# Rotation of the dilated heads moved from VectorE to GpSimd, their transposes moved one attention unit later

## The chip, the cores and the metric

The kernel runs on one core of a Trainium2 chip. The metric is the device time of one execution in microseconds, as the median of several executions. Five engines work side by side, each through its own list of instructions: TensorE (PE in the profile), VectorE (DVE), ScalarE (ACT), GpSimd (POOL) and SyncE (SP, which here only issues transfers). They meet through semaphores: an instruction with a wait holds up all that is queued behind it on its engine.

## What is computed

Two blocks on a sequence of 256 tokens and 1024 channels in float32. The change lies in the first, which has two layers. Of each layer the part that matters is this (cut from the reference):

```python
for layer in range(DEPTH):                      # DEPTH = 2
    h = rmsnorm(x, norm_mix[layer])
    z = h @ w_in[layer]                         # 256 x 2964
    ...                                         # z is split into the inputs of four mixers
    o_a = nsa_mixer(...); o_b = diff_mixer(...); o_c = mlstm_mixer(...)
    o_d = dilated_mixer(heads(d_q), heads(d_k), heads(d_v), cos64, sin64)
    x = x + jnp.concatenate([o_a, o_b, o_c, o_d], axis=-1) @ w_out[layer]
    ...                                         # feed-forward part

def dilated_mixer(q, k, v, cos, sin):
    q = apply_rope(q, cos, sin)                 # x1*cos - x2*sin, x1*sin + x2*cos
    k = apply_rope(k, cos, sin)
    ...                                         # masked attention with counted keys
```

The second block (convolutions, routing, experts) is not touched.

## The kernel before

The 256 tokens are two tiles of 128 rows. z is made in six pieces (chunks) of up to 512 columns. For each, TensorE multiplies both tiles; ScalarE takes tile 0 out of PSUM (`z_act`) and VectorE takes tile 1 (`z_dve`). The last piece, `C_DIL`, holds the queries and keys of the dilated mixer: 2 x 4 heads of 64 columns.

Attention is a software pipeline over 14 units, `u` = 0 to 13: 4 to 7 are the differential mixer, 8 and 9 the window part of the NSA mixer, 10 and 13 its compressed part, 11 and 12 the dilated mixer (`U_DIL` = 11). There is no scheduler: the order on each engine is that of the code. In step `u`

- TensorE transposes the probabilities of unit u (L585, L587; waits `probs` and `o_done` of the unit before), does a piece of other work in `ahead_of_values` (products of z, L522, and from step 9 on the output product, L618), multiplies by the values (L602), makes the scores of unit u+2 (L570), and does `behind_scores`;
- ScalarE copies the transposed probabilities of unit u+1 out of PSUM (`transposed_out`, L867 to L871) and takes the exponentials of unit u+2 (L856);
- VectorE turns exponentials into the factors of unit u+1 (`probabilities`, L1096 to L1133), takes the output of unit u (`unit_out`, L1146 to L1157) and masks the scores of unit u+2 and finds their maxima (`masked`, L1046 to L1051).

The dilated heads take a way through all of them. VectorE rotates tile 0 of them at the end of step 6 and tile 1 at the end of step 7, in `rotate_dil` (L381 to L386, four instructions per tile), and raises `rope`. TensorE transposes them behind the scores of step 8 (`dil_batch`, eight transposes at L545, waiting for `rope`), and ScalarE copies the result out of PSUM at the end of its step 8 (`qk(B_DIL, ...)`, L839) and raises `prep_ev`. The scores of unit 11, made in step 9, wait for that copy.

GpSimd has little to do in this stage: it rotates the heads of the differential mixer (`rotate_diff`, the same function `rotate` with the same 128x512 sizes) when their piece of z is there, and then waits for the end of attention to issue small transfers (`ada_bias`, `params`).

Of the kernel before, what the change touches and what calls it, by code (L numbers as in the profile page):

```python
# [394 lines left out]
def first_pool(nc, pool, m, a):  # L395
# [28 lines left out]
    def rotate_diff(L):  # L424
# [7 lines left out]
            last = rotate(nc.gpsimd, pool, m, m.rz_b, m.tmp_pool, i, [(z_heads(m, i, Z_BQ, 16, 32), 0, 16, 32)])  # L432
        last.then_inc(s["rope_b"], 1)

    params(0)
    pool.wait_ge(m.consts_in, 16 * m.n_consts)
    for L in range(DEPTH):
        rotate_diff(L)
        ada_bias(L)
        if L < DEPTH - 1:  # L440
            params(L + 1)
# [51 lines left out]
def first_tensor(nc, pe, m):  # L493
# [5 lines left out]
    for L in range(DEPTH):  # L499
# [203 lines left out]
        def dil_batch():  # L703

            pe.wait_ge(s["rope"], nth(L, "rope", 3))
            pe.wait_ge(s["OT"], nth(L, "OT", 1))
            pairs(batch(B_DIL), [cols(m.rz_d, k * P) for k in range(4)]).then_inc(s["prep_ps"], 1)

        def ahead_of_values(u):

            if u < 4:
                z_part(C_VALUES, u // 2, u % 2)
            elif u < 8:
                z_part(C_DIL, u // 2 - 2, u % 2)
            elif u == 8:
                pe.wait_ge(s["o_final"], nth(L, "o_final", 1))
                out_transposes(0)
            elif u == 9:
                pe.wait_ge(m.ring_full[5], (L * 2 + 2) * 16)
                pe.wait_ge(m.ring_full[2], (L * 2 + 2) * 16)  # L720
                z_taken(C_DIL)
                out_ready(0)
                out_part(0, 4)
            elif u == 10:
                pe.wait_ge(s["prep_ev"], nth(L, "prep_ev", N_PREP))
                out_part(1, 4)
            elif u == 11:
                out_ready(1)
                out_part(0, 2)
            elif u == 12:  # L730
                out_part(1, 2)
            else:
                out_ready(2)
                out_part(0, 0)
                out_transposes(3)

        def behind_scores(u):

            if u == 1:
                diff_batch()  # L740
            elif u == 2:
                cmp_batch()
            elif u == 3:
                kv_batch()
            elif u == 8:
                dil_batch()
            elif u == 10:
                pe.wait_ge(s["o_final"], nth(L, "o_final", 2))
                out_transposes(1)
            elif u == 12:  # L750
                pe.wait_ge(s["masked"], nth(L, "masked", N_UNITS))
                out_transposes(2)
# [62 lines left out]
def first_scalar(nc, act, m):  # L815
# [5 lines left out]
    for L in range(DEPTH):  # L821
# [102 lines left out]
        for u in range(N_UNITS):  # L924
            if u == 1:
                z_out(C_VALUES)
            if u == 5:
                z_out(C_DIL)
                head_root(0)
            if u == 8:  # L930
                out_taken(0)
            if u == 9:
                head_root(1)
            if u == 10:
                out_taken(1)
            if u == 12:
                out_taken(2)
            if u + 1 < N_UNITS:
                transposed_out(u + 1)
            if u + 2 < N_UNITS:  # L940
                exponentials(u + 2)
            if u == 1:
                qk(B_DIFF, T_BQ, 4)
            if u == 2:
                rows = m.ps[0:CMP_ROWS, 6, 0:2 * HD].rearrange("n (a e) -> n a e", a=2)
                for x in range(2):
                    evac(B_CMP, m.cmp_u[0:CMP_ROWS, :, x, :], rows)
                evac(B_CMP, m.cmp_u[32:32 + CMP_ROWS, :, 0, :], m.ps[32:32 + CMP_ROWS, 6, 0:2 * HD].rearrange("n (a e) -> n a e", a=2)).then_inc(s["prep_ev"], 1)
            if u == 3:
                evac(B_KV, m.kcT[:, 0:N_CMP], m.ps[:, 6, 0:N_CMP])  # L950
                evac(B_KV, m.vc[0:N_CMP, :], m.ps[0:N_CMP, 7, 0:HD]).then_inc(s["prep_ev"], 1)
            if u == 8:
                qk(B_DIL, T_DQ, 4)
        out_taken(3)
        out_taken(4)

# [23 lines left out]
def first_vector(nc, dve, m):  # L980
# [8 lines left out]
    for L in range(DEPTH):  # L989
# [198 lines left out]
                last = tt(sub, sub, m.z[:, :, Z_O:Z_O + GW], ALU.mult)  # L1188
            last.then_inc(s["o_final"], 1)

        def rotate_dil(i):
            return rotate(v, dve, m, m.rz_d, m.tmp_dve, i, [(z_heads(m, i, Z_DQ, 8, HD), 0, 8, HD)])

        dve.wait_ge(s["small_ready"], nth(L, "small_ready", 1))
        probabilities(0)
        masked(1)
# [3 lines left out]
        for u in range(N_UNITS):  # L1200
            if u + 1 < N_UNITS:
                probabilities(u + 1)
            if u == 3:
                z_out(C_VALUES)
            if u == 7:
                z_out(C_DIL)
            unit_out(u)
            if u + 2 < N_UNITS:
                masked(u + 2)
            if u == 4:  # L1210
                sub_squared(0)
            if u == 5:
                sub_scaled(0)
            if u == 6:
                dve.wait_ge(s["z_act"], nth(L, "z_act", C_DIL + 1))
                rotate_dil(0)
            if u == 7:
                dve.drain()
                rotate_dil(1).then_inc(s["rope"], 1)
            if u == 8:  # L1220
                sub_squared(1)
            if u == 9:
                sub_scaled(1)
# [1410 lines left out]
```

## Time and profile before

| what | value |
|---|---|
| median of 3 runs | 2112.6 us (2111.42 to 2115.61) |
| the profiled execution | 2113.28 us, of which 2111.4 us are the span of the instructions |
| TensorE busy | 1957.8 us (93%) |
| VectorE busy | 658.9 us (31%) |
| ScalarE busy | 315.2 us (15%) |
| GpSimd busy | 84.9 us (4%) |
| granted clock of TensorE over the span | 0.975 of full speed |
| attention steps 6 to 13, layer 0 | about 130 to 190 us |
| the same, layer 1 | about 561 to 620 us |

The profile is of one execution. A span's start is time zero of every view. "Idle before" names the engine whose event ended a wait. A row that merges instructions gives the time from the first one's start to the last one's end, and neighbouring TensorE rows overlap by some tenths of a microsecond, since matmuls are pipelined.

### The profile page before, as it was taken

The numbers are of one execution on the slowest core, as the hardware profiler recorded it, in microseconds if no ns is written. First come the engines' busy times: TensorE is split into PE (matmuls) and PEld (weight loads), VectorE is DVE, ScalarE is ACT, GpSimd is POOL, SyncE is SP. The second block draws the span as 40 slices with busy tenths as digits, with TensorE's granted clock in tenths as the row PEclk, the third lists the DMA queues.
The fourth block names the chain that finished last, engine by engine and source line by source line (L and its number), as shares of the span: only waits on it lengthen the run. The fifth ranks groups of instructions, "written<-read, shape, count | busy, mean of one in ns | idle before, by whom it ended". The sixth has DMA issues, their size and how long they took to land.

```text
span 2111.4 us, 21989 instructions
## 1 busy us (share of the span) xinstructions
PE 1957.8 (93%) x8546; PEld 1080.5 (51%) x8546; DVE 658.9 (31%) x1270; ACT 315.2 (15%) x741; POOL 84.9 (4%) x127
## 2 busy tenths in 40 slices
PE   8988999999889999899999999999899998899886
PEld 4555777755557777674444434443684333233222
DVE  1463434324643433474311111111424211111103
ACT  2442000014430000203111011110101100000000
POOL 3102000001020000200000000000000000000000
PEclk9999999999999999999999999999999999999999
DMA  9215777643148786517699999999536799999995
GB/s 310 74 61 167 260 261 273 221 149 86 61 130 301 246 283 228 196 45 299 256 378 426 428 426 428 427 428 419 218 130 268 311 424 428 427 428 427 428 426 242
DMA packets 158898, 603.07 MB, mean 286 GB/s; under 512 B 16776, under 2 KB 73016, under 8 KB 128080
## 3 DMA queue, kind: packets, MB, share of 16 engines
q1 hardware_dynamic: 153728, 591.43, 71.8%
q0 software_dynamic: 4880, 10.22, 1.8%
q8 instruction: 69, 1.13, 0.2%
q14 instruction: 29, 0.24, 0.0%
q10 hardware_dynamic: 192, 0.05, 0.0%
HBM read 597.67 MB, written 1.10 MB: 284 GB/s over the span
## 4 chain that ended last, share of the span: by engine, by line
PE 73%; DMA 17%; DVE 5%; issue 2%; ACT 1%; DVEq 1%; ACTq 1%; SPq 0%
PE ps L1986 15%; PE ps L790 15%; DMA ring<-in_e_w_up 8%; DMA ring<-in_e_w_gate 7%; PE ps L796 7%; PE ps L522 7%; PE ps L2004 5%; PE ps L1820 4%; PE ps L1785 3%; PE ps L1914 3%; PE ps L1833 3%; PE ps L1929 3%; PE ps L618 2%; DMA ring<-in_e_w_down 1%; PE ps L587 1%
## 5 line engine op out<-in xcount | busy, mean ns | idle before, releaser
L790 PE MATMUL ps<-hT,ring 128*128 128x256 f32 x1408 | 314.1, 384 | 1.5 <-DVE hT L284 1.5
L790 PEld LDWEIGHTS ps<-hT,ring 128*128 128x128 f32 x1408 | 277.5, 198 | 34.1 <-issue 4.0
L1986 PE MATMUL ps<-ring,hT 128*64 128x512 f32 (+1 forms) x1024 | 231.3, 604 | 30.7 <-DMA ring<-in_e_w_up 15.8
L1986 PE MATMUL ps<-ring,late 128*64 128x512 f32 (+1 forms) x960 | 213.6, 597 | 20.0 <-DMA ring<-in_e_w_up 11.3
L2004 PE MATMUL ps<-ring,qkT 128*64 128x512 f32 (+1 forms) x1024 | 226.6, 594 | 5.8 <-ACT qkT L2201 4.5
L522 PE MATMUL ps<-ring,hT 128*128 128x512 f32 (+1 forms) x384 | 170.1, 594 | 3.1 <-DMA ring<-in_w_in 2.3
L1986 PEld LDWEIGHTS ps<-ring,hT 128*64 128x64 f32 (+1 forms) x1024 | 72.9, 125 | 185.2 <-issue 185.2
L796 PE MATMUL ps<-ring,late 128*128 128x512 f32 x352 | 154.7, 592 | 0.0
L1986 PEld LDWEIGHTS ps<-ring,late 128*64 128x64 f32 (+1 forms) x960 | 66.3, 124 | 160.9 <-issue 160.9
L2004 PEld LDWEIGHTS ps<-ring,qkT 128*64 128x64 f32 (+1 forms) x1024 | 68.6, 123 | 145.1 <-issue 145.1
L1269 DVE SCALAR_TENSOR_TENSOR qkT<-ring,cc,qkT 128x512 f32<-128x512 f32 x168 | 125.9, 749 | 10.3 <-issue 0.4
L2462 DVE TENSOR_TENSOR qkT<-ps,qkT 128x512 f32<-128x512 f32 (+1 forms) x64 | 44.2, 690 | 267.4 <-PE ps L2004 267.4
L522 PEld LDWEIGHTS ps<-ring,hT 128*128 128x128 f32 x384 | 73.1, 197 | 80.4 <-issue 70.7
L1290 DVE TENSOR_TENSOR late<-ps,late 128x256 f32<-128x256 f32 x44 | 18.7, 425 | 296.6 <-ACT late L972 296.6
L2483 DVE TENSOR_TENSOR qkT<-ps,qkT 128x512 f32<-128x512 f32 (+1 forms) x32 | 22.1, 690 | 280.8 <-PE ps L1986 280.8
L796 PEld LDWEIGHTS ps<-ring,late 128*128 128x128 f32 x352 | 66.9, 190 | 74.6 <-issue 73.7
L1914 PE MATMUL ps<-qkT 128*128 128x512 f32 x192 | 95.2, 618 | 0.0
L1929 PE MATMUL ps<-qkT,O 128*128 128x256 f32 x384 | 92.6, 381 | 2.1 <-DVEq L2443 2.1
L2479 DVE TENSOR_TENSOR x<-ps,x 128x1024 f32<-128x1024 f32 x24 | 29.4, 1225 | 196.5 <-PE ps L1914 196.5
L1820 PE MATMUL ps<-hT,ring 128*128 128x256 f32 x384 | 85.0, 384 | 1.6 <-DVE hT L2253 0.9
L972 ACT ACTIVATE late<-ps 128x256 f32<-128x256 f32 x44 | 16.9, 384 | 445.8 <-PE ps L790 445.8
L1929 PEld LDWEIGHTS ps<-qkT,O 128*128 128x128 f32 x384 | 70.3, 190 | 25.5 <-issue 14.6
(379 smaller groups left out, 1693.8 us busy)
## 6 DMA issues: line engine op xcount, KB each, us to landing
ring<-in_e_w_down SPq DMA_DIRECT2D x64, 2048.0 KB, 16.1
ring<-in_e_w_up SPq DMA_DIRECT2D x64, 2048.0 KB, 17.3
ring<-in_e_w_gate SPq DMA_DIRECT2D x60, 2048.0 KB, 17.1
ring<-in_ada_w SPq DMA_DIRECT2D x24, 2048.0 KB, 10.4
ring<-in_w_gate SPq DMA_DIRECT2D x22, 1024.0 KB, 7.5
ring<-in_w_up SPq DMA_DIRECT2D x22, 1024.0 KB, 9.9
ring<-in_w_down SPq DMA_DIRECT2D x22, 1024.0 KB, 11.7
ring<-in_w_in SPq DMA_DIRECT2D x8, 2048.0 KB, 14.3
```

Of the source, the lines that this page charges most:

```text
L522: last = mm(m.ps[:, 4 + i, 0:chunk_width(n)], m.hT[:, j, i * P:(i + 1) * P], w[:, j, :], start=(j == 0), stop=(j == KC - 1))
L790: last = mm(m.ps[:, c, at:at + SEQ], w[:, j, c, :], m.hT[:, j, :], start=(j == 0), stop=(j == KC - 1))
L796: last = mm(m.ps[:, 4 + 2 * i + n2, :], m.ucT[:, c, i * P:(i + 1) * P], wd[:, c, n2 * 512:(n2 + 1) * 512], start=(u == 0 and c == 0), stop ...
L1269: last = stt(acc, w, m.cc[:, j:j + 1], acc, ALU.mult, ALU.add)
L1785: last = mm(m.ps[:, c % 4, half * SEQ:(half + 1) * SEQ], w[half][:, j, at:at + P], m.hT[:, j, :], start=(j == 0), stop=(j == KC - 1))
L1820: last = mm(dst, w[half][:, j, at:at + P], m.hT[:, j, :], start=(j == 0), stop=(j == KC - 1))
L1833: last = mm(m.ps[:, 4 + 2 * i + n, :], vT[:, j, i * P:(i + 1) * P], w[:, j, :], start=(j == 0), stop=(j == KC - 1))
L1914: last = mm(m.ps[:, 6 + n, :], m.GwT[:, i, :], half_of(m.ye, n), start=True, stop=True)
L1929: last = mm(m.ps[:, k % depth, n * SLOTS:(n + 1) * SLOTS], hN, m.G[l][:, i].rearrange("p x s -> p (x s)"), start=(i == 0), stop=(i == 1))
L1986: last = mm(dst, xg[:, j, at + x * n_tok:at + (x + 1) * n_tok], w(x, j), start=(j == 0), stop=(j == KC - 1))
L2004: lasts[x] = mm(dst, m.hidT[:, j, rows + x * n_tok:rows + (x + 1) * n_tok], half_of(w(x, j), n), start=(j == 0), stop=(j == 3))
L2462: tt(half_of(m.ye[rows], n), m.ps[rows, 4 + n, :], half_of(m.gf[rows], n), ALU.mult).then_inc(t["ye"], 1)
```

## The change

GpSimd gets a function `rotate_dil`, which stands right behind `rotate_diff`: it waits for both tiles of the piece `C_DIL` and rotates tile 0 and tile 1. VectorE loses its eight instructions per layer in steps 6 and 7. TensorE does `dil_batch` in step 9 behind the first part of the output product and ahead of the values, instead of at the end of step 8. ScalarE copies its result in step 9 behind `head_root(1)` (the square root of the sums of squares of the differential output) and ahead of `transposed_out(10)`.

```diff
@@ first_pool
+    def rotate_dil(L):
+
+        pool.wait_ge(s["z_act"], nth(L, "z_act", C_DIL + 1))
+        pool.wait_ge(s["z_dve"], nth(L, "z_dve", C_DIL + 1))
+        for i in range(TILES):
+            last = rotate(nc.gpsimd, pool, m, m.rz_d, m.tmp_pool, i, [(z_heads(m, i, Z_DQ, 8, HD), 0, 8, HD)])
+        last.then_inc(s["rope"], 1)
...
     for L in range(DEPTH):
         rotate_diff(L)
+        rotate_dil(L)
         ada_bias(L)
@@ first_tensor
                 out_ready(0)
                 out_part(0, 4)
+                dil_batch()
...
-            elif u == 8:
-                dil_batch()
@@ first_scalar
             if u == 9:
                 head_root(1)
+                qk(B_DIL, T_DQ, 4)
...
-            if u == 8:
-                qk(B_DIL, T_DQ, 4)
@@ first_vector
-        def rotate_dil(i):
-            return rotate(v, dve, m, m.rz_d, m.tmp_dve, i, [(z_heads(m, i, Z_DQ, 8, HD), 0, 8, HD)])
...
-            if u == 6:
-                dve.wait_ge(s["z_act"], nth(L, "z_act", C_DIL + 1))
-                rotate_dil(0)
-            if u == 7:
-                dve.drain()
-                rotate_dil(1).then_inc(s["rope"], 1)
```

TensorE, from the scores made in step 8 to those made in step 9, before:

```order
L570 MATMUL ps<-kcT,qkT 128x15 [waits prep_ev,masked]
L570 MATMUL ps<-kcT,qkT 128x15 x3
L545 MATMUL ps<-ident,qkT 128x128 [waits prep_ev,OT,rope]
L545 MATMUL ps<-ident,qkT 128x128 x7
L587 MATMUL ps<-ident,ring 128x128 [waits probs,o_done]
L587 MATMUL ps<-ident,ring 128x128 x7
L618 MATMUL ps<-ring,hT 128x512 [waits z_dve,z_act,OT,ring_full2,ring_full5]
L618 MATMUL ps<-ring,hT 128x512 x3
L602 MATMUL ps<-z,ring 128x64 [waits pt]
L602 MATMUL ps<-z,ring 128x64 x7
L570 MATMUL ps<-qkT 128x128 [waits prep_ev,masked]
```

The same place in the changed kernel, where the lines stand nine further down (L554 is `dil_batch`, L596 the transposes of the probabilities, L627 the output product, L611 the values):

```order
L579 MATMUL ps<-kcT,qkT 128x15 [waits prep_ev,masked]
L579 MATMUL ps<-kcT,qkT 128x15 x3
L596 MATMUL ps<-ident,ring 128x128 [waits probs,o_done]
L596 MATMUL ps<-ident,ring 128x128 x7
L627 MATMUL ps<-ring,hT 128x512 [waits z_dve,z_act,OT,ring_full2,ring_full5]
L627 MATMUL ps<-ring,hT 128x512 x3
L554 MATMUL ps<-ident,qkT 128x128 [waits prep_ev,OT,rope]
L554 MATMUL ps<-ident,qkT 128x128 x7
L611 MATMUL ps<-z,ring 128x64 [waits pt]
L611 MATMUL ps<-z,ring 128x64 x7
L579 MATMUL ps<-qkT 128x128 [waits prep_ev,masked]
```

The eight transposes of the dilated heads moved behind those of the probabilities and the eight products.

ScalarE, from the last exponentials of unit 10 to the exponentials of unit 11, before:

```order
L856 ACTIVATE ring,small<-ring,small 128x15 x3
L839 ACTIVATE qkT<-ps 128x1024 [waits prep_ps]
L878 ACT_TABLE_LOAD
L878 ACTIVATE small<-small,eps 128x2x4 [waits ss]
L867 ACTIVATE ring<-ps 15x4x128 [waits pv,pt_ps]
L856 ACT_TABLE_LOAD [waits pt_ps]
```

And in the changed kernel (L847 is the copy, L886 the square root):

```order
L864 ACTIVATE ring,small<-ring,small 128x15 x3
L886 ACT_TABLE_LOAD
L886 ACTIVATE small<-small,eps 128x2x4 [waits ss]
L847 ACTIVATE qkT<-ps 128x1024 [waits prep_ps]
L875 ACTIVATE ring<-ps 15x4x128 [waits pv,pt_ps]
L864 ACT_TABLE_LOAD [waits pt_ps]
```

The copy of the dilated heads moved behind the square root.

## Rows read from the trace of the kernel before

**Rows 1.** Page, part 1: busy time, share of span, weight of TensorE.

```profile
PE 1957.8 (93%) x8546; PEld 1080.5 (51%) x8546; DVE 658.9 (31%) x1270; ACT 315.2 (15%) x741; POOL 84.9 (4%) x127
```

**Rows 2.** Chain of waits, layer 0, steps 7 to 9: start us, us, what.

```profile
139.58 0.69 DVE qkT L381
...
141.01 0.70 DVE qkT L386
...
142.39 1.35 PE ps L545 x8
...
149.44 1.75 PE ps L602 x16
...
151.28 0.42 DVE late L1153
```

**Rows 3.** Timeline of VectorE, layer 0: start us, us, engine line op, idle before.

```profile
134.81 0.75 DVE L1002 TENSOR_SCALAR z<-ps,small 128x512 f32<-128x512 f32 x1
...
141.80 0.18 DVE L1096 RECIPROCAL small<-small 128x4 f32<-128x4 f32 x1
142.05 0.16 DVE L1099 TENSOR_TENSOR small<-small,gates 128x4 f32<-128x4 f32 x1
...
142.80 0.43 DVE L1155 TENSOR_TENSOR O<-O,late 128x256 f32<-128x256 f32 x1
```

**Rows 4.** Timeline of ScalarE, layer 0, steps 7 to 9.

```profile
139.52 0.51 ACT L856 ACTIVATE ring<-ring,small 128x256 f32<-128x256 f32 x1 [1.62 <-DVE small L1051]
...
141.41 0.19 ACT L856 ACTIVATION_READ_ACCUMULATOR ring<-ring,small 128x1 f32 x1
...
147.76 1.02 ACT L839 ACTIVATE qkT<-ps 128x1024 f32<-128x1024 f32 x1
...
150.10 0.30 ACT L878 ACTIVATE small<-small,eps 128x8 f32<-128x8 f32 x1
```

**Rows 5.** Timeline of TensorE, layer 0.

```profile
89.30 1.09 PE L545 MATMUL ps<-ident,qkT 128*128 128x128 f32 x8
...
130.68 0.65 PE L587 MATMUL ps<-ident,ring 128*128 128x128 f32 x4 [2.56 <-DVE O L1146]
131.17 3.60 PE L522 MATMUL ps<-ring,hT 128*128 128x512 f32 x8
...
139.54 0.62 PE L570 MATMUL ps<-kcT,qkT 64*128 64x15 f32 x8 [0.49 <-DVE small L1051]
...
167.19 1.97 PE L587 MATMUL ps<-ident,ring 128*128 128x128 f32 x8 [2.43 <-DVE O L1157]
168.95 4.29 PE L618 MATMUL ps<-ring,hT 128*128 128x512 f32 x8
```

**Rows 6.** Windows: stretch, length, busy of PE, PEld, DVE, ACT, POOL, then PEclk.

```profile
143.00:143.50 0.50, 0.50 (x5) 0.50 (x3) 0.43 (x3) 0.00 (x0) 0.00 (x0) 0.53 0.86 350
...
146.00:146.50 0.50, 0.50 (x2) 0.34 (x1) 0.00 (x0) 0.50 (x2) 0.00 (x0) 0.55 0.00 0
```

**Rows 7.** Timeline of GpSimd: ends of its rotation, layer 0, then layer 1.

```profile
74.41 1.09 POOL L381 TENSOR_TENSOR qkT<-z,late 128x512 f32<-128x512 f32 x1 [36.61 <-DVE z L1002]
...
83.87 1.26 POOL L386 TENSOR_TENSOR qkT<-qkT 128x512 f32<-128x512 f32 x1
...
503.21 1.09 POOL L381 TENSOR_TENSOR qkT<-z,late 128x512 f32<-128x512 f32 x1 [309.58 <-DVE z L1002]
...
511.05 1.26 POOL L386 TENSOR_TENSOR qkT<-qkT 128x512 f32<-128x512 f32 x1
```

**Rows 8.** Timeline of VectorE: one instruction, beside GpSimd's rotation and behind it.

```profile
82.23 0.97 DVE L1046 TENSOR_TENSOR ring<-ring,late 128x512 f32<-128x512 f32 x1 [0.30 <-PE ps L570]
...
512.45 0.69 DVE L1046 TENSOR_TENSOR ring<-ring,late 128x512 f32<-128x512 f32 x1 [0.30 <-PE ps L570]
```

**Rows 9.** Timelines of layer 1: TensorE at the batch, VectorE at the output.

```profile
572.84 1.69 PE L545 MATMUL ps<-ident,qkT 128*128 128x128 f32 x8 [2.23 <-DVE qkT L386]
...
573.25 0.42 DVE L1155 TENSOR_TENSOR O<-O,late 128x256 f32<-128x256 f32 x1
```

## The prediction, made before the changed kernel was run

> **What bounds the kernel now.** The page's engine table comes first: TensorE is busy for 1957.8 of 2111.4 us and VectorE for 658.9 [rows 1]. So work taken off VectorE gains only where TensorE waits for it. The change touches one place of each of the two layers, and there I read the chain of waits. In layer 0 it goes through the second rotation on VectorE (139.58 to 141.71), then the eight transposes of the dilated heads (142.39), then TensorE's own work up to the end of the values (149.44 + 1.75), and from there to the output of unit 9 on VectorE (151.28) [rows 2]. The timelines of the engines show what runs beside that chain, and the windows show TensorE's clock. Layer 1 has the same pattern, 430.45 us later: transposes at 572.84 after the same wait [rows 9].
>
> **Rotation leaves VectorE.** Two tiles per layer; each takes 141.71 - 139.58 = 2.13 us [rows 2]. The first one I cost at nothing: behind it VectorE takes the last piece of z at 134.81, and TensorE only ends its product for it then. The second stands on the chain, so 2.1 us per layer seem to be for the taking. They are not. Beside it ScalarE takes the exponentials of unit 9, from 139.52 to 141.41 + 0.19 = 141.60 [rows 4]. VectorE needs them for the factors of unit 9, which it begins at 141.80 [rows 3]; a handover from one engine to the next I take at 0.09 us, as between the end of the values (149.44 + 1.75 = 151.19) and the output at 151.28 [rows 2], so without the rotation they begin at 141.69. The gain for what follows on VectorE is **0.11 us**.
>
> **TensorE's work moves later.** Before, TensorE ends the scores of unit 10 at 139.54 + 0.62 = 140.16 [rows 5] and waits for the rotation until 142.39 [rows 2]. The transposes of the dilated heads then fill the rest of the time until VectorE has taken the output of unit 8, at 142.80 + 0.43 = 143.23 [rows 3], for which the transposes of the probabilities wait. In the changed kernel those come first, so TensorE starts when that output is there: 143.23 - 0.11 + 0.09 = **143.21**, against 142.39. All of its work from here to the end of the values is the same, in another order: 8 + 8 transposes, 8 products, 16 products with values. Nothing in it waits (below), so the end moves by as much as the start, **+0.82 us** at an equal clock. In layer 1 the output of unit 8 ends at 573.25 + 0.42 = 573.67 [rows 9], the start is 573.65 against 572.84, so +0.81.
>
> **The clock makes that a little less, or more.** TensorE's granted clock falls to its lower level (1.2 of 2.4 GHz, 0.53 as a mean of the half microsecond) at about 143.0 after the wait, and is low until about 146.4, where the mean is 0.55 [rows 6]. If the low stretch keeps its place, start time lost inside it counts half: layer 0 loses 0.64 at full clock up to 143.03 and half of 0.18 behind it, together 0.7; layer 1, where the eight transposes took 1.69 instead of 1.09 [rows 5, 9] and so ran low almost from their start, 0.5. Together 1.2 us in place of 1.6. But the wait grows from 2.2 to 3.0 us. A fall is no matter of course: a wait of 2.56 us at 130.68 is followed by products at full pace (3.60), one of 2.43 at 167.19 by transposes of 1.97 and products of 4.29 [rows 5]. A fall costs 4.29 - 3.60 + 1.97 - 1.09 = **1.6 us**. This place pays it already in both layers; executions in which it does not will mostly pay it after the change. I add nothing for it in the sum and 1.6 us per layer in the range.
>
> **GpSimd beside VectorE.** GpSimd starts when VectorE has taken the last piece of z, 134.81 + 0.75 [rows 3], plus the handover, at 135.65. The same rotation took it 85.13 - 74.41 = 10.72 us in layer 0 and 512.31 - 503.21 = 9.10 in layer 1 [rows 7]. So it ends between 144.8 and 146.4, and it overlaps the factors and the output of unit 8 on VectorE. The nearest row for what that costs: a VectorE instruction with two operands in SBUF took 0.97 us beside a GpSimd instruction and 0.69 when GpSimd had finished [rows 8], so 0.28. On the new path two such instructions stand in a row: the factors times the gates (142.05) and the sum into O (142.80) [rows 3]. Bounds for each: nothing, and the longest GpSimd instruction, 1.26 us [rows 7]. I take 0.28 for each, the one row there is, 0.56 per layer, partly in the low clock: **+0.4 us** per layer. The maskings of steps 7 and 8 have one operand in PSUM; that they aren't slowed is assumed, and no row shows it.
>
> The Trainium skill, "SBUF — State Buffer", section "Who interferes with whom", says that a VectorE instruction with two SBUF inputs contends with a GpSimd instruction that reads SBUF, and that whichever comes second blocks until the first is done. This trace agrees in direction with its 0.28 us; how long a full block is, no row shows. Taken at its word, two blocks per layer could come to 2.5 us, which is the slower rival below.
>
> **Does the new place make anybody wait?** TensorE reaches the moved transposes after the output product. Before, the values began at 149.44 [rows 2], with the transposes already done; 1.09 us of them [rows 5] now stand there instead. TensorE reaches them at 149.44 + 0.73 - 1.35 = 148.8 at the earliest (1.35 is what they took before). GpSimd is done by 146.4: a cover of 2.4 us. ScalarE's copy must be there before the scores of unit 11, which follow the values. ScalarE is through with the exponentials of unit 10 by 147.7; the square root takes until 150.40 - 148.78 = 1.62 us later, 149.3, and shifts with the rest by under 1 us; the transposes end at 150.0 to 151, and the values behind them at 151.8 to 152.8; the copy takes 1.02 [rows 4], while TensorE does the values for 1.75. That leaves 0.7 to spare, so nothing. GpSimd's next jobs wait for the end of attention and aren't late; SP's queue is passed by nothing.
>
> **Sum.** Layer 0: 0.7 + 0.4; layer 1: 0.5 + 0.4; together **+2.0 us**. From 151.28 on the chain of waits goes to the end of attention with no gap that a shift of this size could fill, and the feed-forward stage behind it is TensorE's, so the shift stays. The profiled execution's 2113.28 would be 2115.3; it lies 0.7 above the median of 2112.6, so the median is forecast at **2114.5 us** (2112.6 + 2.0, rounded to a half).
>
> **Rivals.**
> - The rotation's time is gained: the chain itself speaks for it, as it goes through the second rotation and 0.68 us behind it. Then 2 x 2.2 = 4.4 us go, 2108.2. Against it are the exponentials, which end 0.11 us before the rotation. Chance 0.04.
> - The clock is kinder: the later start shifts every following wait of TensorE, and some that now end in a fall of the clock (167.19) no longer do. One fall less is -1.6 us, two -3.2: 2111.3 to 2112.9. For it: the 2.56 us wait without a fall. Against it: it may as well go the other way. Chance 0.14.
> - Slower: GpSimd blocks VectorE for whole instructions at both places. The start of TensorE moves from 143.21 by 1.26 + 1.09 [rows 7] to 145.56, a loss of 3.2 us per layer at full clock (the low stretch then lies behind the start as well), 6.4 in both: 2119.0. It decides from 2112.6 + 4.2, so from 2.1 us per layer, which is 1.3 us of blocking over the two instructions. For it: GpSimd is busy in most of that stretch. Against it: the one such row shows 0.28. Chance 0.12.
> - GpSimd comes too late for the transposes: it would have to take over 13 us instead of 9.1 to 10.7, and each further microsecond costs one per layer. With 3 us more, 2112.6 + 2.0 + 2 x 0.5 to 2 x 1.5, 2115.5 to 2117.5. Chance 0.05.
>
> **How the numbers follow.** The forecast has 0.65. A measurement of this kernel can tell about 0.2% (4.2 us) from no change, as the three runs before spread over that much. The forecast, the kind clock and most of the late GpSimd lie within it: 0.83. Slower holds the blocking rival and a tail of the late one and of clock falls on top of the forecast: 0.13. Faster holds the first rival: 0.04. The range goes from the kind clock with one or two falls less, 2111.2, to just short of the blocking rival, which includes one fall more on top of the forecast plus the spread, 2117.8.
>
> **What would show it.** In the profile of the changed kernel: VectorE idle between its maxima of step 7 and the factors of unit 9, released by ScalarE (about 2.2 us); TensorE's wait ahead of the transposes of step 9 at 3.0 us or more, released by the sum into O; the moved transposes and the scores of unit 11 with no wait; the output of unit 9 beginning 0.7 to 1.5 us later than before; GpSimd's rotation 9 to 11 us long. Wrong I am if the factors or the sum into O of step 8 take over 1 us each, if TensorE waits for GpSimd or for ScalarE's copy, or if the output of unit 9 comes earlier than before.

## The result and the profile after

The changed kernel is slower by a quarter of a per cent: its median is 2117.6 us (15 runs, 2114.26 to 2122.72) against 2112.6 us of the kernel before, 1.0023 times as long, with an interval of 1.0016 to 1.0031. A second measurement, made with the last experiments, gave the same: 2118.25 us against 2112.28, 1.0023 (1.0015 to 1.0032). The forecast was 2114.5 us. The time lies in the range, at its upper edge; the sign is the one forecast; the size, 5.0 us instead of 2.0, is not.

The engine table after the change, in the columns of [rows 1]:

```profile
PE 1968.1 (93%) x8546; PEld 1083.8 (51%) x8546; DVE 652.2 (31%) x1254; ACT 314.9 (15%) x741; POOL 98.6 (5%) x143
```

GpSimd took over sixteen instructions (x127 to x143, 13.7 us), VectorE has sixteen fewer, and TensorE is busy for 10.3 us more **with the same 8546 instructions**. That is the first thing to see: the same instructions took longer, and the windows below show them at a lower clock. But 7.0 of the 10.3 us lie in the second block (1141.4 us busy before, 1148.5 after), whose length hardly changed (1241.0 and 1241.2 us); the sum over the span does not say what the change costs.

The chain of waits at the changed place of layer 0 (start, us, what), to be laid beside [rows 2]:

```profile
142.23 0.88 DVE O L1162
...
143.16 1.97 PE ps L596 x8
145.12 5.31 PE ps L627 x8
150.44 0.87 PE ps L554 x8
151.31 1.75 PE ps L611 x16
```

The second rotation has left the chain, as was meant. In its place stands the sum into O of unit 8 on VectorE, and the eight products of L627 take 5.3 us of it. The timeline of TensorE there (start, us, engine, line, operation, idle before), to be compared with [rows 5]:

```profile
139.11 0.62 PE L579 MATMUL ps<-kcT,qkT 64*128 64x15 f32 x8 [0.48 <-DVE small L1058]
143.16 1.97 PE L596 MATMUL ps<-ident,ring 128*128 128x128 f32 x8 [3.43 <-DVE O L1162]
144.92 5.52 PE L627 MATMUL ps<-ring,hT 128*128 128x512 f32 x8
150.27 1.04 PE L554 MATMUL ps<-ident,qkT 128*128 128x128 f32 x8
```

and the same stretch in the kernel before:

```profile
142.39 1.35 PE L545 MATMUL ps<-ident,qkT 128*128 128x128 f32 x8 [2.23 <-DVE qkT L386]
143.54 1.91 PE L587 MATMUL ps<-ident,ring 128*128 128x128 f32 x8
145.24 4.20 PE L618 MATMUL ps<-ring,hT 128*128 128x512 f32 x8
```

The wait grew from 2.23 to 3.43 us and the products from 4.20 to 5.52 (eight of the same size take 3.60 at full clock, [rows 5]). The windows give the clock (stretch, length, busy us of PE, PEld, DVE, ACT and POOL, then PEclk, the granted clock), here of the changed kernel:

```profile
141.50:142.00 0.50, 0.00 (x0) 0.00 (x0) 0.41 (x2) 0.36 (x1) 0.45 (x1) 0.95 1.14 363
142.00:148.50 6.50, 5.34 (x13) 3.27 (x14) 3.73 (x12) 3.26 (x10) 0.82 (x1) 0.50 0.44 173
148.50:149.00 0.50, 0.50 (x3) 0.18 (x2) 0.13 (x1) 0.49 (x2) 0.00 (x0) 0.73 0.00 0
...
575.50:578.50 3.00, 2.52 (x9) 2.10 (x10) 2.31 (x6) 0.52 (x1) 0.14 (x1) 0.50 0.69 281
578.50:579.00 0.50, 0.50 (x2) 0.33 (x1) 0.00 (x0) 0.50 (x2) 0.00 (x0) 0.65 0.00 0
```

In layer 0 TensorE was at its lower level (0.50, 1.2 of 2.4 GHz) from 141.95 to 148.77: a mean of 0.95 over half a microsecond is 0.05 us of it low, one of 0.73 is 0.27. That is 6.8 us, where the kernel before had 3.4, from 143.03 to 146.45 [rows 6]. In layer 1 the fall comes at 575.44 and the rise at 578.85, 3.4 us, as before.

The same happens a second time, further down in layer 1, at a wait whose length did not change. Changed kernel:

```profile
600.52 1.97 PE L596 MATMUL ps<-ident,ring 128*128 128x128 f32 x8 [2.43 <-DVE O L1164]
602.28 5.53 PE L627 MATMUL ps<-ring,hT 128*128 128x512 f32 x8
```

Kernel before:

```profile
597.64 1.97 PE L587 MATMUL ps<-ident,ring 128*128 128x128 f32 x8 [2.44 <-DVE O L1157]
599.40 4.11 PE L618 MATMUL ps<-ring,hT 128*128 128x512 f32 x8
```

**Where the 5.3 us between the two spans (2116.7 and 2111.4) are.** I measure from the start of one row to the start of another, in both profiles. "At the place" is from the scores of unit 10 to the output of unit 9. "Low" is for how long the granted clock was 0.50 in the stretch, before and after.

| stretch | before | after | difference | low |
|---|---|---|---|---|
| at the place, layer 0 | 11.74 | 14.04 | +2.30 | 3.4, 6.8 |
| at the place, layer 1 | 11.73 | 12.67 | +0.94 | 3.4, 3.4 |
| masking of unit 11 to first feed-forward product, layer 1 | 47.90 | 49.31 | +1.41 | 6.1, 11.5 |
| first feed-forward product of layer 1 to TensorE's first work of the second block | 239.99 | 240.74 | +0.75 | 4.1, 5.5 |
| ahead of the place, layer 0 | 139.54 | 139.11 | -0.43 | 10.2, 6.8 |

Together 4.97; the stretches that are left add 0.3, none of them more than that. The second profile of the changed kernel (r1_after, below) gives 14.05, 12.67, 49.30 and 240.76. The second profile of the kernel before (r2_before) has 11.72, 11.73, 47.97 and 240.08, so these four do not hang on one execution.

Other stretches do. From the first piece of z of layer 1 to the scores of unit 10 the kernel before took 127.16 us in one profile, with 10.2 us of low clock, and 124.18 in the other, with 3.4. And in layer 0, from the masking of unit 11 to the first feed-forward product, r2_before took 49.50 us where the first profile of the same kernel took 47.95 and the changed kernel 47.80 and 47.85. So the kernel before meets the lengthening of the third row too, only in the other layer and not in every execution. The wait is again that of step 11 (r2_before):

```profile
167.26 1.97 PE L587 MATMUL ps<-ident,ring 128*128 128x128 f32 x8 [2.44 <-DVE O L1157]
169.02 5.71 PE L618 MATMUL ps<-ring,hT 128*128 128x512 f32 x8
```

### The profile page after: what moved, and what is told of

It reads as the page before. It is cut to its first block, busy times and chain, and to the rows that moved or that the text cites. A ratio compares the mean times of both kernels' runs of the same rounds, so it can differ in the third digit from the quotient of the medians.

```text
span 2116.7 us, 21989 instructions
## 1 busy us (share of the span) xinstructions
PE 1968.1 (93%) x8546; PEld 1083.8 (51%) x8546; DVE 652.2 (31%) x1254; ACT 314.9 (15%) x741; POOL 98.6 (5%) x143
## 4 chain that ended last, share of the span: by engine, by line
PE 73%; DMA 17%; DVE 5%; issue 2%; ACT 1%; DVEq 1%; ACTq 1%; SPq 0%
PE ps L1984 16%; PE ps L798 15%; DMA ring<-in_e_w_gate 11%; PE ps L804 7%; PE ps L531 7%; PE ps L2002 5%; DMA ring<-in_e_w_up 4%; PE ps L1818 4%; PE ps L1783 3%; PE ps L1912 3%; PE ps L1831 3%; PE ps L1927 3%; PE ps L627 2%; DMA ring<-in_e_w_down 1%; PE ps L611 1%
## 5 line engine op out<-in xcount | busy, mean ns | idle before, releaser
L1984 PE MATMUL ps<-ring,hT 128*64 128x512 f32 (+1 forms) x1024 | 237.4, 618 | 25.5 <-DMA ring<-in_e_w_up 13.7
```

The lines of the kernel that those rows point to most:

```text
L1984: last = mm(dst, xg[:, j, at + x * n_tok:at + (x + 1) * n_tok], w(x, j), start=(j == 0), stop=(j == KC - 1))
```

## The experiments

Each was compared with the kernel before on the same chip, in 8 to 12 runs. "Place" is the length at the place in layer 0 and layer 1, 11.74 and 11.73 us before. "Low" is how long the granted clock was 0.50 there, added up from windows of half a microsecond or one.

| kernel | median us | before us | ratio and interval | place us | low us |
|---|---|---|---|---|---|
| e1_engine | 2115.7 | 2112.0 | 1.0020 (1.0011 to 1.0029) | 12.64, 12.59 | 3.4, 3.4 |
| e2_order | 2119.0 | 2112.0 | 1.0032 (1.0022 to 1.0041) | 12.97, 13.97 | 6.8, 6.8 |
| e3_psum | 2117.2 | 2112.0 | 1.0022 (1.0013 to 1.0031) | 12.20, 12.46 | 3.4, 3.4 |
| e4_warm | 2111.1 | 2112.0 | 1.0000 (0.9991 to 1.0009) | 11.33, 11.30 | 0, 0 |
| e5_warm_before | 2110.1 | 2112.7 | 0.9990 (0.9981 to 0.9999) | 10.11, 10.11 | 0, 0 |
| e6_warm_order | 2113.1 | 2112.7 | 0.9997 (0.9987 to 1.0007) | 10.99, 10.99 | 0, 0 |
| f1_fill_dve | 2110.4 | 2112.7 | 0.9992 (0.9981 to 1.0003) | 8.74, 8.73 | 0, 0 |
| f2_fill_pool | 2111.2 | 2112.7 | 0.9992 (0.9981 to 1.0003) | 10.43, 8.75 | 3.4, 0 |
| f3_copy_first_dve | 2110.0 | 2112.3 | 0.9989 (0.9981 to 0.9998) | 8.74, 8.73 | 0, 0 |
| f4_copy_first_pool | 2106.2 | 2112.3 | 0.9970 (0.9959 to 0.9981) | 8.75, 8.74 | 0, 0 |
| r1_after | 2118.3 | 2112.3 | 1.0023 (1.0015 to 1.0032) | 14.05, 12.67 | 6.8, 3.4 |
| r2_before | 2112.4 | 2112.3 | 0.9997 (0.9988 to 1.0006) | 11.72, 11.73 | 3.4, 3.4 |

### One part of the change alone

**e1_engine**: GpSimd rotates, but transposes and copy stay in step 8.

```diff
@@ first_tensor, ahead_of_values, step 9
-                dil_batch()
@@ behind_scores
+            elif u == 8:
+                dil_batch()
@@ first_scalar: qk(B_DIL, T_DQ, 4) from step 9 back to the end of step 8
```

> The changed kernel with the eight transposes and their copy put back into step 8; only the rotation is on GpSimd. My theory (the cost is that TensorE starts its work of steps 8 and 9 later, and that the longer wait lengthens the low stretch of its clock): the transposes wait for GpSimd, which in the changed kernel's trace ends 7.5 us after VectorE has taken z, so TensorE starts 0.9 us later than before in each layer; 2115 to 2117 us. Rival (GpSimd beside VectorE is the cause): as slow as the changed kernel, near 2117.5, with the sum into O blocked by 0.4 us again, though here it stands beside the transposes and not ahead of them. Rival (the order is the whole cause): as before, 2112.6.

The wait is now for GpSimd itself, and this is its row on TensorE:

```profile
139.96 1.97 PE L554 MATMUL ps<-ident,qkT 128*128 128x128 f32 x8 [3.15 <-POOL qkT L386]
```

The start moved by 0.93 us against before (139.96 - 136.18 = 3.78, against 2.85), and the place grew by 0.90 and 0.86. The engine alone makes TensorE late, and that costs. The sum into O, beside GpSimd's last instruction, is as slow here as in the changed kernel:

```profile
139.30 0.88 DVE L1164 TENSOR_TENSOR O<-O,late 128x256 f32<-128x256 f32 x1
```

TensorE has no wait behind it: the transposes of the dilated heads fill the time until it is done. So this cost comes from GpSimd's late end and not from the contention. The place accounts for 1.8 of the 3.7 us between the medians.

**e2_order**: the other part. VectorE rotates, in steps 6 and 7 as before; transposes and copy move to step 9. Against the kernel before:

```diff
@@ first_tensor, step 9, behind out_part(0, 4)
+                dil_batch()
@@ behind_scores
-            elif u == 8:
-                dil_batch()
@@ first_scalar: qk(B_DIL, T_DQ, 4) from step 8 to step 9, behind head_root(1)
```

> The kernel before with only the order changed: the eight transposes and their copy in step 9, the rotation still on VectorE. My theory: TensorE waits for the sum into O of unit 8 at 143.23 in the time of before, so it starts 0.9 us later per layer; with the longer low stretch of the clock 2115 to 2117 us, nearly all of the change's cost, and no instruction of VectorE longer than before. Rival (GpSimd is the cause): 2112.6, as before.

```profile
144.19 1.97 PE L587 MATMUL ps<-ident,ring 128*128 128x128 f32 x8 [3.13 <-DVE O L1153]
145.96 4.74 PE L618 MATMUL ps<-ring,hT 128*128 128x512 f32 x8
```

The wait is 3.13 us, and the products take 4.74 us here and 5.76 in layer 1. The start moved by 0.90, the place by 1.23 and 2.24, and the low stretch is 6.8 us long in both layers. The order alone is at least as dear as the whole change. So the loss needs neither GpSimd nor a contention: it comes with the wait that the order leaves open. The two parts do not add up (0.20 and 0.32% alone, 0.23% together), as each lengthens the same wait. The time is 2 us over what was expected, and the profile has a doubled low stretch in both layers, which the expectation did not reckon with.

### Does GpSimd block VectorE?

**e3_psum**: the changed kernel, but in unit 8 the product of output and factors stays in PSUM, so the sum into O has only one operand in SBUF.

```diff
-                    tmp = m.ucT[:, 0, :].rearrange("p (h d) -> p h d", d=HD)
+                    tmp = src4 if u == 8 else m.ucT[:, 0, :].rearrange("p (h d) -> p h d", d=HD)
```

> The changed kernel, but in unit 8 the product of output and factors stays in PSUM, so that the sum into O has one operand in SBUF and one in PSUM. If GpSimd blocks VectorE instructions with two operands in SBUF, the sum falls from 0.87 back to some 0.43 us and TensorE starts 0.4 us earlier in each layer: 0.8 to 1.2 us less than the changed kernel, some 2116.5. If it is contention of another kind, the sum stays at 0.87.

The rows of VectorE in the changed kernel, then in e3_psum:

```profile
141.73 0.42 DVE L1160 TENSOR_TENSOR late<-ps,small 128x256 f32<-128x256 f32 x1
142.23 0.87 DVE L1162 TENSOR_TENSOR O<-O,late 128x256 f32<-128x256 f32 x1
```

```profile
142.16 0.43 DVE L1160 TENSOR_TENSOR ps<-ps,small 128x256 f32<-128x256 f32 x1
142.66 0.42 DVE L1162 TENSOR_TENSOR O<-O,ps 128x256 f32<-128x256 f32 x1
```

The sum took 0.87 us instead of the 0.43 of [rows 3], and 0.42 with its second operand in PSUM. TensorE's wait shrank by 0.45 (3.43 to 2.98), the place by 1.84 and 0.21 us; the 1.84 came with a low stretch of 3.4 us in place of 6.8. The median did not follow: 1.0022 against 1.0023. The 0.8 to 1.2 us that were expected are less than the half-width of these intervals (1.6 to 1.9 us), so the medians can't tell whether they came. What the run shows is that the contention is real, and that the change costs about as much without it.

### Is it the clock?

**e4_warm**: the changed kernel, with 22 transposes of the identity in TensorE's wait. They write into a part of PSUM that `dil_batch` overwrites before ScalarE copies it, and are work in addition.

```diff
@@ behind_scores
+            elif u == 8:
+                dst = batch(B_DIL)
+                for n in range(WARM):          # WARM = 22
+                    nc.tensor.transpose(dst[:, 512:512 + P], m.ident[:], m.ident[:])
```

> The changed kernel with 22 additional transposes of the identity into an unused PSUM bank behind the scores of step 8, some 2.9 us of work that nobody reads, in TensorE's wait of 3.4 us. My theory has a part of the cost in the granted clock: no low stretch follows, the eight transposes take 1.0 instead of 2.0 us and the products 3.6 instead of 4.2 to 5.5, so 1.6 to 2.9 us less per layer than in the changed kernel: 2111.5 to 2114.5. Rival (the clock is no part of it, only the start): as the changed kernel, 2117.5.

```profile
137.00 2.62 PE L759 MATMUL ps<-ident 128*128 128x128 f32 x22
140.53 1.09 PE L597 MATMUL ps<-ident,ring 128*128 128x128 f32 x8 [0.92 <-DVE O L1167]
141.46 3.60 PE L628 MATMUL ps<-ring,hT 128*128 128x512 f32 x8
```

The windows of 137 to 150 us in the changed kernel and in e4_warm; the column behind POOL is the granted clock:

```profile
137.00:150.00 13.00, 8.84 (x35) 5.47 (x34) 6.38 (x17) 6.91 (x21) 5.39 (x6) 0.74 0.64 227
```

```profile
137.00:150.00 13.00, 11.64 (x78) 8.73 (x77) 6.60 (x18) 7.47 (x21) 3.05 (x4) 1.00 0.42 151
```

The useful work starts as late as in the changed kernel (140.53 - 136.44 = 4.09 us behind the scores, 4.05 in the changed kernel), yet it runs at full clock: 1.09 and 3.60 in place of 1.97 and 5.52. The whole kernel is back at the time of before, 1.0000. Only TensorE's idleness was changed, so **all of the loss can be given back by keeping TensorE busy in this wait**. That does not yet say that the loss was all clock: the transposes also save the fall that the kernel before pays here. For that the kernel before has to be filled as well.

**e5_warm_before**: the same in the kernel before, 16 of them ahead of `dil_batch()`.

```diff
             elif u == 8:
+                dst = batch(B_DIL)
+                for n in range(WARM):          # WARM = 16
+                    nc.tensor.transpose(dst[:, 512:512 + P], m.ident[:], m.ident[:])
                 dil_batch()
```

> The kernel before with 16 additional transposes of the identity into an unused PSUM bank in its own wait of 2.2 us in step 8. If the granted clock is what such a wait costs, the kernel before pays it too, for about 3.4 us at half speed per layer: 1.6 us less per layer, 2109 in place of 2112. If the clock fell for another reason, nothing changes.

```profile
139.97 1.06 PE L546 MATMUL ps<-ident,qkT 128*128 128x128 f32 x8 [0.34 <-issue]
...
141.78 3.60 PE L619 MATMUL ps<-ring,hT 128*128 128x512 f32 x8
```

The place takes 10.11 us, 1.6 less per layer: the price of a fall as the prediction had it, which the kernel before pays here too. Of these 3.2 us the median shows 2.7 (0.9990). Filled against filled, the changed kernel is still 1.22 and 1.19 us longer at the place (11.33 and 11.30 against 10.11), which is its later start, and 0.10% slower (1.0000 against 0.9990, with intervals that touch). By these rows about 2.4 of the 5.0 us are the later start at full clock; at the place the clock adds 0.8 (2.30 + 0.94 - 2.4), and the rest came further down.

**e6_warm_order**: e2_order with the 22 transposes of e4_warm.

```diff
@@ behind_scores, against e2_order
+            elif u == 8:
+                dst = batch(B_DIL)
+                for n in range(WARM):          # WARM = 22
+                    nc.tensor.transpose(dst[:, 512:512 + P], m.ident[:], m.ident[:])
```

> The reordered kernel with the rotation on VectorE (e2_order) and 22 additional transposes of the identity in its wait. e2_order took 2119.0. My theory: the later start alone costs 0.9 us per layer and the clock the rest, so this one comes to about 2111, as e4_warm did, though its transposes of step 9 start 0.9 us later than in the kernel before. Rival (the place of the eight transposes ahead of the values costs by itself, without the clock): 2114 or more.

```profile
143.25 1.09 PE L588 MATMUL ps<-ident,ring 128*128 128x128 f32 x8 [0.57 <-DVE O L1158]
144.17 3.60 PE L619 MATMUL ps<-ring,hT 128*128 128x512 f32 x8
```

1.0032 becomes 0.9997: the dearest of the variants is repaired by the same means, without GpSimd. The 2113.1 us lie between the 2111 expected and the rival's 2114; the place is 10.99 against 10.11 in e5_warm_before, so the 0.9 us per layer of later start are still there.

### Useful work in the wait

**f1_fill_dve**: dummy work shows the cause but does nothing. The first part of the output product needs only what is there in the wait, so here it moves ahead, into step 8, and the transposes take its place in step 9. Against the kernel before:

```diff
@@ ahead_of_values, step 9
-                pe.wait_ge(m.ring_full[5], (L * 2 + 2) * 16)
-                pe.wait_ge(m.ring_full[2], (L * 2 + 2) * 16)
-                z_taken(C_DIL)
-                out_ready(0)
-                out_part(0, 4)
+                dil_batch()
@@ behind_scores, step 8: the five lines stand here, in place of dil_batch()
@@ first_scalar
-            if u == 8:
-                out_taken(0)
             if u == 9:
                 head_root(1)
+                qk(B_DIL, T_DQ, 4)
...
+            if u == 7:
+                out_taken(0)
...
-            if u == 8:
-                qk(B_DIL, T_DQ, 4)
```

> Real work in place of the additional transposes: the kernel before with the first part of the output product (8 products, 3.4 us) moved into the wait of step 8, the eight transposes of the dilated heads in step 9, and ScalarE's copy of the first transposed outputs ahead of the exponentials of unit 9, so that the product has its operand. The wait of TensorE goes to under 0.5 us and no low stretch follows: the output of unit 9 comes 3 to 3.7 us earlier per layer than before, 2104 to 2107. Rival (something on VectorE or ScalarE takes the place of the wait at once): over 2109.

**f2_fill_pool**: the same edit in the changed kernel, with GpSimd rotating.

```diff
@@ as in f1_fill_dve, against the changed kernel: the five lines from step 9 to behind_scores of
   step 8, and out_taken(0) from step 8 to step 7
```

> The same move of the output product in the changed kernel, so with the rotation on GpSimd. TensorE no longer waits for the sum into O of unit 8, so GpSimd's 0.4 us on it are hidden as well as VectorE's rotation is in f1_fill_dve: the same time as f1_fill_dve within 1 us. If the engine of the rotation matters by itself, they differ by over 2 us.

The product covers the wait, and the place shrinks to 8.7 us; only in layer 0 of f2 it is 10.43, since there the clock fell at 141.66, in the middle of the product (5.40 us for it), with no wait of over half a microsecond in the stretch. Both medians come out within the measurement of before (0.9992 twice), over 3 us above the 2104 to 2107 expected of f1: its rival, that another engine takes the place of the wait at once, is what happened. Part of the gain is given back in the timeline of TensorE of f1_fill_dve:

```profile
137.97 3.70 PE L618 MATMUL ps<-ring,hT 128*128 128x512 f32 x8
...
147.50 0.92 PE L570 MATMUL ps<-qkT 64*128 64x128 f32 x8 [1.84 <-ACT qkT L839]
148.35 1.03 PE L585 MATMUL ps<-ident,ring 128*15 128x128 f32 x4
149.17 4.65 PE L618 MATMUL ps<-ring,hT 128*128 128x512 f32 x8
```

The scores of unit 11 wait 1.84 us for ScalarE's copy, since on ScalarE the square root stands ahead of it:

```profile
144.85 1.28 ACT L878 ACT_TABLE_LOAD   x1
146.14 0.30 ACT L878 ACTIVATE small<-small,eps 128x8 f32<-128x8 f32 x1
146.35 1.00 ACT L839 ACTIVATE qkT<-ps 128x1024 f32<-128x1024 f32 x1
```

That new wait brings a clock fall of its own (4.65 against 3.60).

**f3_copy_first_dve** and **f4_copy_first_pool**: f1 and f2 with the copy ahead of the square root.

```diff
             if u == 9:
+                qk(B_DIL, T_DQ, 4)
                 head_root(1)
-                qk(B_DIL, T_DQ, 4)
```

> f1_fill_dve with ScalarE's copy of the dilated heads ahead of the square root instead of behind it. In f1's trace the scores of unit 11 wait 1.84 us for that copy, which stands behind a table load and the square root (1.6 us), and the clock falls behind that wait. My theory: the wait is gone, unit 11's masking begins 9.6 us after the scores of unit 10 in place of 11.0 (12.6 before), no low stretch follows; 3 us per layer less than before, 2105 to 2107. Rival (the wait only moves on, to the transposed probabilities of unit 10 behind the square root): the masking comes early, but the time stays at 2110.

> The same swap in f2_fill_pool, so with the rotation on GpSimd: the same as f3_copy_first_dve within 1 us. A difference of over 2 us would say that the engine of the rotation matters once TensorE's wait is filled.

The timeline of TensorE in f4_copy_first_pool:

```profile
140.13 3.70 PE L627 MATMUL ps<-ring,hT 128*128 128x512 f32 x8
...
148.21 0.72 PE L579 MATMUL ps<-qkT 64*128 64x128 f32 x8 [0.37 <-ACT qkT L848]
149.31 0.61 PE L594 MATMUL ps<-ident,ring 128*15 128x128 f32 x4 [0.39 <-DVE O L1163]
149.76 3.60 PE L627 MATMUL ps<-ring,hT 128*128 128x512 f32 x8
```

No row of the stretch is low, and its longest wait is 0.39 us. f4_copy_first_pool is the one kernel that clearly beats both: 2106.2 us, 0.9970 (0.9959 to 0.9981). f3_copy_first_dve gains only 0.11%, though the place takes the same 8.74 us in it. Expected were 2105 to 2107 for it, and f4 within 1 us of it; they are 3.7 us apart, which by the expectation would say that the engine of the rotation matters. The profiles don't show how: they differ by 2.0 us, at other places, and there by the clock. From the first piece of z of layer 1 to the scores of unit 10 f3 takes 127.1 us with 10.2 us of low clock, f4 123.9 with 3.4; but the kernel before does both, in its two profiles. From the masking of unit 11 to the first feed-forward product f3 takes 49.37 us in layer 1 and f4 47.88, while in layer 0 it is 47.94 against 49.37, the other way. Over the whole span both have 105 us of low clock. Whether the 3.7 us are the engine or where the falls happened to come is open; the intervals of the two ratios touch. What is shown is the place: 3.0 us per layer for both.

**r1_after** and **r2_before** are the changed kernel and the kernel before once more, each against the kernel before, with nothing edited; r2_before is at the same time the test of the measurement.

> The changed kernel itself again, beside the others on the same chip. From the scores of unit 10 to the output of unit 9 it should again take 12.6 to 14.1 us against 11.7 in the kernel before, varying with the length of the low stretch, and the time should be 3 to 7 us over before. Rival (the first profile's double low stretch was chance, the usual cost is 0.9 per layer): both layers at 12.6.

> The kernel before itself, for a second profile of it: the time within 1 us of before. By my theory one low stretch of the clock follows the wait in step 8 in each layer, 11.7 us from the scores of unit 10 to the output of unit 9; where none does, 10.1 us, as with the additional transposes.

1.0023 and 0.9997: the loss repeats, and a difference of 0.03% is nothing.

## Why the prediction was right, and where it was not

**Rotation leaves VectorE: right.** VectorE has nothing to do where the second rotation stood, and waits for ScalarE's exponentials. Its row in the changed kernel:

```profile
141.22 0.18 DVE L1103 RECIPROCAL small<-small 128x4 f32<-128x4 f32 x1 [2.17 <-ACTq L865]
```

2.17 us were idle, "about 2.2" forecast. The rival "the rotation's time is gained" falls with this row.

**TensorE's work moves later: right.** For the start, 0.82 us plus 2 x 0.28 for GpSimd was forecast, 1.38. From the start of the scores of unit 10 to the start of TensorE's work it was 2.85 us [rows 2, 5] and is 143.16 - 139.11 = 4.05, so +1.20; in layer 1 it is 575.98 - 571.94 = 4.04.

**GpSimd beside VectorE: the size near, the places not.** I took 0.28 for each of two instructions. The sum into O alone paid, 0.44 (0.87 against 0.43). The factors times the gates took 0.16 us, as before, but they began at 141.47, in the pause between two of GpSimd's instructions, so they tell nothing of the contention. The product out of PSUM, L1160, took 0.42 beside a busy GpSimd, which was assumed. Blocking for a whole instruction, twice per layer, did not come. GpSimd's own rows:

```profile
135.28 1.09 POOL L381 TENSOR_TENSOR qkT<-z,late 128x512 f32<-128x512 f32 x1 [50.82 <-DVE z L1009]
...
140.77 0.64 POOL L383 TENSOR_TENSOR qkT<-z,late 128x256 f32<-128x256 f32 x1
141.56 1.26 POOL L386 TENSOR_TENSOR qkT<-qkT 128x512 f32<-128x512 f32 x1
```

It was through at 142.82, after 7.5 us instead of 9 to 11, so only its last instruction met the sum. That one had begun 0.67 us ahead of the sum and ended 0.59 behind the sum's start. The sum lost 0.44. The row from which the prediction took its 0.28 is of the same kind: VectorE's instruction began at 82.23 [rows 8], in the kernel before, while this one of GpSimd was running:

```profile
81.99 0.66 POOL L382 TENSOR_TENSOR qkT<-z,late 128x256 f32<-128x256 f32 x1
```

0.42 us of it were left, and 0.28 were lost. In both cases VectorE lost what was left of GpSimd's instruction, less 0.14 or 0.15 us. So 0.28 was no price of a meeting as such: it hangs on when the second one comes, and the near agreement of 0.44 with the 0.56 forecast is in part luck.

The Trainium skill, "SBUF — State Buffer", section "Who interferes with whom", says that the instruction that comes second blocks until the first is done, and that, outside VectorE's 2-port modes, only a second operand in SBUF brings VectorE into it. The runs agree on the second point (e3_psum: 0.42 with an operand in PSUM). They agree with the first about in size: what was lost follows the remainder of GpSimd's instruction (0.44 of 0.59 us, 0.28 of 0.42), not its whole length.

**The new place makes nobody wait: right.** The moved transposes and the scores of unit 11 have no wait in their rows. In the faster order of f1_fill_dve the copy behind the square root did become late. The cover that the prediction counted (0.7 us) was this one, and a place shorter by 3 us used it up.

**The clock: here the sum failed.** The prediction had the mechanism in hand: the fall, its price of 1.6 us, and that the wait would grow from 2.2 to 3.0 us. Then it said "I add nothing for it in the sum", and it rested its 1.2 us on "If the low stretch keeps its place". In layer 1 that came out nearly: the stretch was as long as before and began 0.54 us ahead of TensorE's first transpose, so that 578.85 - 575.98 = 2.87 us of the work ran low instead of 3.4, and the place lost 0.94 where 0.5 + 0.4 was forecast. In layer 0 the stretch doubled: 148.77 - 143.16 = 5.61 us of work ran low instead of 3.4. Half of the difference is 1.1, and that is what the work behind the wait lost: 153.15 - 143.16 = 9.99 us against 151.28 - 142.39 = 8.89 [rows 2]. So the terms of the sum at the place came to 2.30 and 0.94 against 1.1 and 0.9. The 1.6 us that I kept for the range were the price of one fall more; what came was one stretch of twice the length, which I had not thought of. So the step that was mis-sized is this term: nothing in the sum for the clock beyond the 1.2 us, where the low stretch took another 1.1 us in layer 0.

**Two terms stood in no sum.** A wait of the same length in step 11 of layer 1 (2.43 us) was followed by a low stretch of 6.8 us in place of 3.4 in both profiles of the changed kernel, with products of 5.5 us in place of 4.1: +1.4. But r2_before has 6.8 us and products of 5.7 at the same wait of layer 0, so it is open how much of this the change brought. In the changed kernel:

```profile
599.50:606.00 6.50, 5.48 (x13) 3.42 (x14) 2.35 (x11) 2.18 (x9) 0.00 (x0) 0.50 0.01 3
```

The rival "the clock is kinder" had said that a later start may change what follows a later wait, "as well go the other way"; it did, and I gave that direction only the tail. The product over all its 128 instructions, before and after (busy us, mean ns of one):

```profile
L618 PE MATMUL ps<-ring,hT 128*128 128x512 f32 x128 | 59.7, 613 | 0.9 <-ACT hT L884 0.9
```

```profile
L627 PE MATMUL ps<-ring,hT 128*128 128x512 f32 x128 | 63.1, 642 | 0.9 <-ACT hT L892 0.9
```

3.4 us more for the same work. It is not a firm size: the second profile of before has 61.0. e4_warm is back at 59.7.

The other term, +0.75 between the first feed-forward product of layer 1 and the second block, is clock as well. The low stretch that begins at the wait ahead of it, at 627.7 us before and at 630.1 after, reaches into the products: 4.1 us of it before, 5.5 after. Less half of its low time the length is 237.9 or 238.0 us in both, and 237.9 in e4_warm (240.43, 5.0 low) and e5_warm_before (240.71, 5.6 low), which are no slower than before.

**Right in part by luck.** The place gave 3.2 us instead of 2.0. That the median, 5.0 us up, still lies in the range is owed to the room that was kept for one fall more and for the spread; it lies 0.2 us under the top, and the later waits that helped to bring it there stood in no sum.

**What stays open.** Which other waits end in a low stretch of 3.4 us, of 6.8, or in none changes between kernels that differ only ahead of them, and in part between two executions of one kernel: ahead of 60 us there are 3.4 us of low clock in before, none in r2_before, after and r1_after. The low clock of the whole span is 105 and 111 us in the two profiles of before and 128 and 124 in those of the changed kernel. Of this 57 and 67, and 74 and 70, lie in the second block, whose length is the same in all four within 0.5 us. The experiments show that filling this one wait gives the loss back. They don't show how much of it comes through the later waits, which I did not fill one by one.

## What to carry to other kernels

Where TensorE is the bound, work moved out of its wait is not free, even if its sum stays the same: transposes that end a wait early also keep the engine from standing still, and here 1.2 us of later start per layer came with 5 us in the median. Count the price of a clock fall as a term, with a doubled low stretch as its dear case, wherever an edit makes a wait of TensorE longer. And before taking work off the engine that TensorE waits for, look for work of TensorE itself that can go into the wait: that was worth 3.0 us per layer at the place, once the copy it needs stood ahead of a table load.

## What the runs showed of the hardware

- **A low stretch of TensorE has more than one length.** It was 3.4 or 6.8 us at the changed place and in step 11, and nothing between; at the wait of 4.13 us ahead of the feed-forward part of layer 1 it was 6.8 before and 10.2 after the change. A wait of 2.23 us had 3.4; one of 3.43 us in layer 0 had 6.8, but one of 3.42 us in layer 1 had 3.4; one of 2.43 us in step 11 of layer 1 had 3.4 before and 6.8 after the change. The length of the wait alone does not set it. The stretch runs from the fall, also while TensorE still waits, so what it costs is half of what work lies in it. And a filled wait is no promise: in f2_fill_pool the clock once fell inside the filled stretch, at 141.7 us.
- **Work that nobody reads can pay.** 2 x 16 transposes of the identity took 2.7 us (0.10%) off the kernel before, 2 x 22 took all of the loss off the changed one.
- **What VectorE loses beside GpSimd hangs on when it comes.** Instructions with two operands in SBUF lost 0.44 us where 0.59 of GpSimd's instruction was left, and 0.28 where 0.42 was left.
- **GpSimd's time for the same eight instructions varies**: 10.7 and 9.1 us beside the differential heads [rows 7], 7.5 here. Most of the difference is one pause, of 2.78 us in layer 0 and 1.64 in layer 1. The rest in layer 0 is one instruction of 0.65 us that took 1.11; it began at 82.61, beside VectorE's of 82.23 to 83.20 [rows 8], and lost 0.46 where 0.59 was left. The others are equally long.
